# Three feed-forwards of a streaming-encoder trunk by units of seven half products

## The reference

```python
def rms_norm(x, g):
    y = x * lax.rsqrt(jnp.mean(x * x, axis=-1, keepdims=True) + EPS)
    return y * g

def swiglu(h, w_in, w_out):                       # D_FF = 2816
    gu = h @ w_in
    gate, up = gu[..., :D_FF], gu[..., D_FF:]
    return (jax.nn.silu(gate) * up) @ w_out

for l in range(2):
    g = norm_gains[l]
    x = x + 0.5 * swiglu(rms_norm(x, g[0]), ffn_w_in[l, 0], ffn_w_out[l, 0])
    h = rms_norm(x, g[1])
    x = x + (s5_mixer(h, ...) if l == 0 else mla_attention(h, cos, sin, k, v, ...))
    x = x + 0.5 * swiglu(rms_norm(x, g[2]), ffn_w_in[l, 1], ffn_w_out[l, 1])
    if l == 0:
        k, v = shared_kv(x, cos, sin, ...)
return rms_norm(x, final_norm)
```

## Time and profile before

| | |
|---|---|
| runs, median of 3 | 1782.54 us (1782.09 to 1784.65) |
| profiled execution | 1781.33 us, span 1779.5 us, mean granted clock 0.996 |
| PE busy | 1737.3 us (98%), 9321 matmuls |
| weight loads of PE | 1455.0 us (82%) |
| DVE (VectorE) | 1054.8 us (59%) |
| ACT (ScalarE) | 701.5 us (39%) |
| POOL (GpSimd) | 448.1 us (25%) |
| chain that ended last | PE 82%, DVE 8%, ACT 4%, DMA 2%, issue 2% |

### The profile page before, as it was taken

How to read it: one execution, slowest core, us unless ns; L and a number is a source line. 1 busy time by engine, 2 the same in 40 slices (tenths; PEclk the granted TensorE clock), 3 DMA queues, 4 the chain that set the end, 5 groups by cost and what they waited for, 6 DMA issues and landing times.

```text
span 1779.5 us, 23933 instructions
## 1 busy us (share of the span) xinstructions
PE 1737.3 (98%) x9321; PEld 1455.0 (82%) x9321; DVE 1054.8 (59%) x1187; ACT 701.5 (39%) x1008; POOL 448.1 (25%) x360
## 2 busy tenths in 40 slices
PE   9999999998999999999999999999999889999998
PEld 6888877876888888888888888888777689889986
DVE  7878888647455444333474333333774889648953
ACT  6342233347334333332353333322574455325542
POOL 8997273025023000000000000000200445026401
PEclk9999999999999999999999999999999999999999
DMA  5364556698323223322222222223210235335531
GB/s 201 119 172 130 172 154 181 208 311 272 119 83 107 94 94 99 100 95 95 95 95 95 95 101 98 95 95 95 95 36 24 95 131 184 126 129 177 167 127 59
DMA packets 92615, 223.28 MB, mean 125 GB/s; under 512 B 24720, under 2 KB 35088, under 8 KB 91504
## 3 DMA queue, kind: packets, MB, share of 16 engines
q1 hardware_dynamic: 81472, 206.38, 35.7%
q0 software_dynamic: 2592, 13.51, 2.3%
q10 hardware_dynamic: 8464, 2.20, 0.5%
HBM read 198.98 MB, written 23.07 MB: 125 GB/s over the span
## 4 chain that ended last, share of the span: by engine, by line
PE 82%; DVE 8%; ACT 4%; DMA 2%; issue 2%; SPq 1%; POOL 1%; ACTq 0%; DVEq 0%; POOLq 0%
PE bank L2249 26%; PE bank L2251 26%; PE bank L2250 26%; DVE w_split L1618 2%; PE bank L2609 1%; ACT w_split L1064 1%; DVE w_slots L2030 1%; PE bank L2588 1%; DMA s_y<-u_and_y 1%; DVE g_split L1632 0%; ACT x_gained L1095 0%; DMA w_slots_raw<-wout 0%; ACTq L1097 0%; PE bank L2422 0%; DMA s_ops<-ops_out 0%
## 5 line engine op out<-in xcount | busy, mean ns | idle before, releaser
L1618 DVE TENSOR_TENSOR w_split<-w_raw,w_split 128x1024 fp32r<-128x1024 f32 x230 | 326.6, 1425 | 430.4 <-ACT w_split L1064 429.7
L2249 PE MATMUL bank<-h_split,w_split 128*128 128x512 f32 x1152 | 451.7, 392 | 4.0 <-DVE gate L1630 2.0
L2251 PE MATMUL bank<-h_split,w_split 128*128 128x512 f32 x1152 | 448.4, 389 | 0.0
L2250 PE MATMUL bank<-h_split,w_split 128*128 128x512 f32 x1152 | 448.3, 389 | 0.0
L1064 ACT ACTIVATE w_split<-w_raw 128x1024 fp32r<-128x1024 f32 x230 | 242.1, 1058 | 452.4 <-PE bank L2251 444.0
L2249 PEld LDWEIGHTS bank<-h_split,w_split 128*128 128x128 f32 x1152 | 216.3, 188 | 53.0 <-DVE gate L1630 4.1
L2249 PE MATMUL bank<-g_split,w_split 128*128 128x512 f32 x656 | 255.8, 390 | 0.8 <-DVE g_split L1851 0.8
L2251 PE MATMUL bank<-g_split,w_split 128*128 128x512 f32 x656 | 255.2, 389 | 0.0
L2250 PE MATMUL bank<-g_split,w_split 128*128 128x512 f32 x656 | 255.2, 389 | 0.0
L2250 PEld LDWEIGHTS bank<-h_split,w_split 128*128 128x128 f32 x1152 | 216.3, 188 | 45.3 <-issue 1.0
L2251 PEld LDWEIGHTS bank<-h_split,w_split 128*128 128x128 f32 x1152 | 216.3, 188 | 45.2
(11 more groups left out here) (341 smaller groups left out, 2174.8 us busy)
## 6 DMA issues: line engine op xcount, KB each, us to landing
w_raw<-wstream SPq DMA_DIRECT2D x230, 512.0 KB, 3.5
w_slots_raw<-wunit SPq DMA_DIRECT2D x63, 512.0 KB, 3.7
w_slots_raw<-wout SPq DMA_DIRECT2D x22, 512.0 KB, 3.9
op_slot<-s_ops SPq DMA_DIRECT2D x5, 2048.0 KB, 10.9
s_ops<-ops_out SPq DMA_DIRECT2D x16, 512.0 KB, 3.1
op_slot<-s_ops POOLq DMA_DIRECT2D x3, 2048.0 KB, 14.1
w_slots_raw<-wunit SPq DMA_DIRECT2D x21, 256.0 KB, 4.0
s_ops<-c_pow POOLq DMA_DIRECT2D x8, 512.0 KB, 5.2
```

The costliest lines, as they stand in the source:

```text
L1618: tt(W[:, r, 1, :], RAW[:, r, :], W[:, r, 0, :].bitcast(F32), ALU.subtract).then_inc(s_lo, 1)
L2249: mm(bank, hi, x_hi, start=start, stop=True, skip_group_check=True)
L2250: mm(bank, hi, x_lo, start=False, stop=True, skip_group_check=True)
L2251: return mm(bank, lo, x_hi, start=False, stop=True, skip_group_check=True)
```

## The change

FFN0B and FFN1A go by units too, with the same functions, now with the stage s as an argument. Their packs leave the ring's stream. The weights of all three come as `wpair`, `wunit` and `wout`.

The inputs of a stage get places (six of 16 KB across the old input buffer and the first gated tiles) that the stage before doesn't read, so that they and their sums are made while its last tiles run. The gated tiles move with them. The inputs of the key/value product get a buffer of their own.

```diff
-H_PLACE = (2, 3, 0, 1)
+H_PLACE = ((0, 1, 4, 5), (0, 1, 2, 3), (2, 3, 4, 5))
+G_PLACE = (tuple(range(8, 16)) + (24, 25, 26), tuple(range(16, 27)), tuple(range(8)) + (24, 25, 26))
-    H8 = at("h_products", [P, 4, 2, 8, SEQ // 2], F32R, o_h)
+    H8 = at("h_products", [P, 6, 2, 8, SEQ // 2], F32R, o_h)
+    G8 = at("g_tiles", [P, 27, 2, SEQ], F32R, o_h)
+    KVH = at("kv_input", [P, DT, 2, SEQ], F32R, o_g + 32 * K)
```

```diff
-                sp.dma_start(WR[:, s, :, :], wunit[u - 1][:, 512:1536].rearrange("p (q n) -> p q n", q=2)).then_inc(s_ld[s], 16)
-                sp.dma_start(WR[:, s + 1, 1, :], wunit[u - 1][:, 1536:2048]).then_inc(s_up_in[u % 2], 16)
+                sp.dma_start(WR[:, a:a + 2, 1, :], unit_weights(s, u).rearrange("p (q n) -> p q n", q=4)[:, 1::2, :]
+                             ).then_inc(s_ld[a], 16)
...
-            def add_sum3(u):
-
-                pool.wait_ge(s_ld[unit_slot(u, S3)], LOADED[u, S3])
-                tt(raw(u, S3), raw(u, S3), WR[:, unit_slot(u, S3), 0, :], ALU.add).then_inc(s_sum3, 1)
+            def sum3(s, u):
+
+                loaded(s, u, S3)
+                pool.dma_start(raw(u, S3), wunit[units_before(s, u)][:, 1024:1536], accum_op=ALU.add).then_inc(s_sum3[u % 2], 16)
...
                 elif n == 4:
-                    act.wait_ge(s_sum3, u)
-                    act.wait_ge(s_up_in[u % 2], 16 * ((u + 1) // 2))
+                    act.wait_ge(s_sum3[u % 2], third_loaded(s, u))
```

```diff
-            stat(N_IN1B, BK[6])
-            pe.wait_ge(s_t_lo, 4)
-            for u in range(1, 11):
-                unit(u, 1)
+            plain_pair(FFN1B)
+            sums_by_tokens(N_IN1B, BK[6])
+            pe.wait_ge(s_t_lo, 12)
+            unit(FFN1B, 1, BK[6])
+            for u in range(2, 11):
+                unit(FFN1B, u)
...
+            def spread(bank):
+
+                pe.wait_ge(s_rstd, spreads[spread_count[0]] + 1)
+                spread_count[0] += 1
+                for t in range(4):
+                    last = mm(bank[:, t * P:(t + 1) * P], ONES[:], DIAGS[:, t, :], start=(t == 0), stop=True,
+                              skip_group_check=True)
...
+            def first_units(s, n, bank):
+
+                unit_hi(s, 2, 1)
+                copy_fifth(s, 1)
+                unit_hi(s, 2, 2)
+                copy_first(s, 1)
+                root_by_tokens(n)
+                nc.scalar.preload_act_table(ACT.Silu)
+                unit_hi(s, 1, 4)
+                unit_hi(s, 2, 3)
+                act.wait_ge(s_spread, s + 1)
+                nc.scalar.activation(RSTD[:], bank[:], ACT.Copy).then_inc(s_rs, 1)
+                silu(s, 0)
+                copy_first_and_sixth(s, 1)
+                unit_g_hi(s, 0)
```

In front of FFN0B the GLU's steps carry the inputs and their sums along:

```diff
                 if k >= 1:
-                    h_hi(k - 1, G_IN0B, H)
+                    product_input(FFN0B, k - 1)
                     square(N_IN0B, k - 1)
+                if k >= 3 and k % 2 == 1:
+                    t_hi(FFN0B, k // 2 - 1)
...
+            for k in range(1, 7):
+                square_sum(N_IN0B, k)
+            sum1(FFN0B, 1)
+            sum2(FFN0B, 1)
+            pool.wait_ge(s_used, KVD)
+            sum4(FFN0B, 1)
+            square_sum(N_IN0B, 7)
+            first_units(FFN0B)
```

In front of FFN1B all of them follow WO's tiles:

```diff
             for d in range(DT):
                 split(WO, d)
                 if d >= 1:
                     add_wo(d - 1)
-                if 1 <= d <= 4:
-                    product_lo(d - 1)
-                if d == 2:
-                    t_sums(0)
-                if d == 4:
-                    t_sums(1)
-                    t_lo(0)
-                if d == 6:
-                    t_lo(1)
-                    slots_lo("pair", 0)
-                    slots_lo("pair", 1)
+                    product_lo(FFN1B, d - 1)
+                if d >= 2 and d % 2 == 0:
+                    t_sums(FFN1B, d // 2 - 1)
+                if d >= 3 and d % 2 == 1:
+                    t_lo(FFN1B, d // 2 - 1)
+                if d == 5:
+                    slots_lo("pair", FFN1B, 0)
+                if d == 6:
+                    slots_lo("pair", FFN1B, 1)
```

SP's list for the three stages:

```diff
+            sp.wait_ge(s_yp, BLOCKS)
+            load_first(FFN0B, 1)
+            sp.wait_ge(s_lo, KVD)
+            load_pair(FFN0B, 0)
+            load_pair(FFN0B, 1)
+            sp.wait_ge(s_used, KVD - 2)
+            load_first(FFN0B, 2)
+            sp.wait_ge(s_used, KVD - 1)
+            load_sum1(FFN0B, 1)
+            load_sum1(FFN0B, 2)
+            sp.wait_ge(s_used, KVD)
+            load_sum3(FFN0B, 1)
+            second_pair_and_on(FFN0B)
```

1467 lines of the change are left out of this document (783 added, 684 removed).

## The result

The changed kernel takes 1789.33 us at the median of seven runs (1784.73 to 1791.65), the kernel before 1782.54 us at the median of seven (1781.87 to 1784.98): a ratio of 1.0033, 95% interval 1.0023 to 1.0043. It is slower by 0.3%, where 1742 us was forecast. The profiled execution took 1784.73 us (span 1782.9), the least of the seven, 4.6 us under the median.

The account below looks back on a forecast made before the run. TensorE's issued work and its stalls were taken as the bound. Terms -33.6 + 6.2 + 0.6 - 16.6 + 2.5 + 0.5 = -40.4 us from 1781.3 gave 1740.9, with the runs' median 1742 us; range 1731 to 1773.

Parts of the forecast that it names:

- Units: Tiles of two more feed-forwards as units of 10.08 us in place of 10.88: 33.6 us less.
- Middles: Steps from units to output tiles and back lose 3.1 us in each rewritten feed-forward: 6.2 us more.
- Statistic: One-column sums and 128-column matmuls replace one 512-column matmul in two stages: 0.6 us more.
- Last seam: Before the last feed-forward, work queued earlier cuts a loss of 18.9 us to 2.3: 16.6 us less.
- Seam after the gated unit: Before the second feed-forward, a chain of 9 to 14 us against 10.9 + 0.5: 2.5 us more.
- Key/value seam: Behind the key/value projection, 21.8 us of TensorE work covers some 17 us of VectorE's: 0.5 us more.
- Adding transfer: In each unit, a transfer replacing GpSimd's addition lands 5.5 us after issue, within 6.4 us slack: no cost.
- Rival A: The adding transfer's sum lands late in every unit: up to 1776 us, chance 0.14; beyond break-even, 0.12.
- Rival B: Seam after the gated unit loses 18.9 us: 1757 us; if the last seam stays too, 1774; chance 0.16.

Follow-up runs that it names:

- z3: The changed kernel with GpSimd adding the third sum in each part's last unit only, its weight split and the second up addition moved earlier; 1763.17 us.
- x4: The changed kernel with product 7's weights split ahead of the third pack of output weights in each part's last unit; 1790.26 us.
- y3: The changed kernel with the adding transfer undone in all units, GpSimd adding the third sum again; 1784.44 us.
- z4: The changed kernel with three seam lists reordered, GpSimd's unit 2 sums held back, ScalarE's root table and a split earlier, and z3's middles; 1739.6 us, median of four.
- w1: z4 without its edit of ScalarE's list: root's table load behind the first product's copy, unit 1's third split behind the root; 1748.28 us.
- z2: The changed kernel, output projection reordered: VectorE adds to x before splitting weights, ScalarE makes high part before square, pair's split before input sums' split; 1789.53 us.
- x1: The changed kernel with GpSimd's sums and last additions of squares at the seam after the gated unit cut to one column or plain fills; 1779.56 us.
- x3: The changed kernel with additions and input splits of x tiles 5 and 6 taken before the key/value weights' split; 1790.1 us.
- y4: The changed kernel with VectorE's work reordered at all three seams and GpSimd's unit 2 sums held back at the first; 1782.42 us.
- w3: z4 without its three order edits (x tile 6 in the gated unit, key/value seam, output projection); 1754.57 us.
- x2: The changed kernel with VectorE's additions to x ahead of input splits in the output projection, input sums a tile later too; 1795.3 us.

## Why the prediction was wrong

The direction was wrong by the seams and the middles: TensorE waits there for VectorE and ScalarE, which the sum had level with it. "Missed by" goes by the stretches of the profiled execution. By the prediction's items:

1. *Units* (-33.6): right. Ten units and five products take 107.99 us in every stage of the changed kernel, 0.120 us a matmul. The gain is in the trace, and was taken back elsewhere.
2. *Middles* (+6.2, "as in the last stage"): wrong, 16.6 us where 9.3 was reckoned for three feed-forwards: 13.4 in the first five output stretches (against 62.79 us each, or 63.67 with the latents' statistic) and 3.1 in the last, against z3. The step that failed is that the last stage's middle could be copied: there GpSimd added the third sum in 1.28 us, here a transfer brings it after 5.2 (x4), in the one unit per part that wants it 1.5 us sooner than all others. Item 7 worked out its slack for an inner unit only. y3, z3 show it; z3 shows that the order also mattered.
3. *Statistic* (+0.6): the matmuls take 1.7 us (eight sums of one column from 914.67 to 915.48 us, eight of 128 columns from 921.67 to 922.58) where 1.2 was taken for four and four, 0.5 us more for each stage. What the statistic brings with it was not in the sum, and is the larger part: ScalarE's list got two table loads and a root between two splits. Mended in z4, with a split moved too, this is 8.7 us over three seams (w1); in the changed kernel it is part of what items 4 to 6 miss.
4. *Last seam* (-16.6): wrong by 15.2 us. The stretch from the projection's end to the first output product took 126.5 us where 111.3 was forecast. Item 4 began VectorE's list at the projection's end, as if VectorE were level with TensorE there. It was about 10 us behind (tile 5's addition began at 1402.5 us, its bank was ready at 1392.7): each of its steps waits 1.3 us for ScalarE, and input sums and weight splits stand between the additions. Taken out of z4 one at a time, the order there costs 5.4 us, the table edit 4.2 and the hold 2.6; z2 alone, on the changed kernel, didn't shorten the seam. Even z4 takes 116.6 us, 5.3 more than forecast, and waits 3.9 of them for the addition to x. The half clock didn't go because the idle time didn't.
5. *Seam after the gated unit* (+2.5): 10.6 us too low (123.1 us where 112.5 was forecast). "9 to 14 us" named the right instructions with too low a price: four sums took 6.5 us where item 4 has 2 to 5 for them, and the chain from x's addition to the last input split 16.5 us. TensorE stood idle for 7.3 us where 2.5 was taken, lost 1.8 us to the half clock after it and some 2 behind the tables. Eight additions of GpSimd stood in the window, and x1, without their reads, took the idle time away.
6. *Key/value seam* (+0.5): 10.7 us too low. The sum counted VectorE's work there (17 us against 21.8) but not when it may begin: VectorE stood 9.3 us for the key/value weights, loaded only at 874.6 us, with tile 5's addition behind that wait. x3 and y4 show it, and w3 once more: 5.9 us.
7. *Adding transfer* (0): right in the inner units, with a landing of 4.3 us against the 5.5 assumed; wrong in the last ones (item 2). Taking it out of z4 costs 3.6 us, nearly all at the seams, where item 7 didn't look for a gain.

Together, items 4 to 6 missed by 36.5 us and the middles with the end by 7.3: 43.8 us, as much as lies between the span forecast (1739.1) and the changed kernel's (1782.9). **Rival A** (the sum late in every unit) falls: the inner units are 10.08 us long. **Rival B** (seams not cleared) is what happened. For the two seams that it names its price was nearly right: 25.8 us where its far end has 32. What it left out are the key/value seam (10.7 us) and the middles (7.3), so that even its far end (1774) was 15 us short of the median. The signs named for B, several us of idle and a half clock before unit 1, were the ones that came. The mechanism that ended on the slower side, said of A alone, was B with two more places.

z4 is at 1739.6 us, beside the forecast's 1742, with the second feed-forward at 347.3 us where "some 349" was named. That the units are worth their 33.6 us is borne out; that the two totals are so near is in part luck, since z4's middles lose nothing where 9.3 us were reckoned, and its last seam takes 5.3 us and its key/value seam 1.8 more than forecast. Parts taken out of z4 one at a time cost 15.0 (orders), 8.7 (tables), 4.5 (hold) and 3.6 us (transfer); the middles are worth 16.6 by z3.

## What to carry to other kernels

A faster inner loop moves the bound to its ends. For each seam, write down on every engine when its list reaches the seam's first instruction, not only how long the list is, and count what stands behind a late load. Where VectorE and GpSimd both read SBUF in the critical window, add GpSimd's instructions to VectorE's chain; move those not yet wanted behind it. An offload that is free in the steady state is to be checked again at the first and the last turn, where its slack is another. A half clock is priced by the matmuls that run in it, not by its length. And judge an edit by the stretch that it touches, in a kernel whose other stretches stand still from run to run: alone on the changed kernel the output projection's order gave nothing clear, in z4 it was worth 5.4 us.

## What the runs showed of the hardware

- The contention of VectorE with GpSimd costs by the instruction, so short ones suffer most: an input sum of 0.48 us became 1.4 to 2.3 beside additions and ended 0.28 or 0.29 us after one of them in 13 of 14 cases, 1.2 for a weight split became 1.7 (3.42 for two above) to 2.2 (4.49 for two in y4), and GpSimd's own 1.28 became up to 2.4. On both engines it shows as longer instructions, not as idle time before them. A fill of 0.53 us by GpSimd cost VectorE nothing.
- A table load of ScalarE took 1.28 us, and the next instruction began 1.29 to 1.30 us after the load did [the rows of w1 and z4 above]. The Trainium skill (ScalarE: Activation LUTs, "What ACT_TABLE_LOAD costs") adds a drain and comes to about 2.66 us for each switch; these rows show no more than the load.
- An adding transfer of 256 KB from GpSimd lands after 4.3 us at the median, no later than a plain one of the kernel before (4.9), and after 5.2 beside loads of 512 KB in x4.
- At the seams and middles the stretches at the 1.2 GHz level lasted 3.4 to 10.2 us. They came behind idle time, in some executions also behind waits of 2 to 3 us (x2 at 1027 us, x3 at 826), and not behind the changed kernel's wait of 2.4 us at 649. What one costs goes by the matmuls that run in it: 19 at the first seam, 0.21 us each in place of 0.12, make 1.8 us of a half clock of 10.2 us. The changed kernel's runs spread over 6.9 us, z4's, which has few such waits, over 0.6.
